# mLSTM log weights: rows spread over the partitions by DMA through device memory, in place of products on TensorE

## The chip, the cores and the metric

One NeuronCore of one Trainium2 chip runs the whole program. The metric is device time in microseconds (us): three runs of the kernel before took 2686.16, 2692.14 and 2697.73 us, median 2692.14. Engines are named as the profile names them: PE is TensorE, DVE is VectorE, ACT is ScalarE, POOL is GpSimd, SP is SyncE, which here only issues DMAs.

## The reference, cut to what matters

The program is two transformer-like blocks on 512 tokens of 1024 features. The first block has two layers; each begins with an input projection and feeds an mLSTM that runs over 128-token chunks, four heads, forward and backward. Layer 0 works on 768 tokens (512 and a context of 256), layer 1 needs outputs for 512 only. For one chunk and direction the reference computes:

```python
b = jnp.cumsum(fc, axis=-1)
a = b + m[..., None]
Dlog = b[..., :, None] - b[..., None, :] + ic[..., None, :]
Dlog = jnp.where(order, Dlog, -jnp.inf)
m_t = jnp.maximum(a, jnp.max(Dlog, axis=-1))
w_inter = jnp.exp(a - m_t)
s = jnp.einsum('bhtk,bhsk->bhts', qc, kc) * jnp.exp(Dlog - m_t[..., None])
num = w_inter[..., None] * jnp.einsum('bhtk,bhkv->bhtv', qc, C) + jnp.einsum('bhts,bhsv->bhtv', s, vc)
```

The factor `exp(Dlog - m_t)` is a 128 x 128 matrix per head, chunk and direction. Written with source token s on the partitions and target token t along the free dimension, its logarithm is a row in t, `b_t - m_t`, plus a column in s, `i_s - b_s`, plus a mask of 0 or -1e30. "Log weights" below are the row plus the mask; the column comes in as the bias of the exponential.

## The kernel before

**Tiles and stages.** A projection tile is 128 output features: `out = W^T x` over 8 feature tiles, each as three products of split operands (upper and lower halves, `w_hi`, `w_lo`, `XH`, `XL`). POOL splits each weight tile into `w_hi` and `w_lo` from a ring of four `raw` buffers that SP fills. Layer 0 does each tile in two parts, 512 tokens (24 products) and 256 tokens (24 products); layer 1 does tiles outside k and v for 512 tokens only, in two halves of 12 products. `in_projection` writes out by hand, tile by tile, what PE does: tiles 10 to 13 are v, 14 to 17 are q, tiles 18 and up are done in pieces inside the mLSTM. Between tile parts stand transposes, sums for the convolution branch (`conv_sum`: a sum of `AC`, later of its squares `YC`, over partitions) and the log weights. "Tile 15" below is position 15 of this order.

**Log weights.** `mlstm_steps(l)` lists 12 pairs of direction and chunk in each layer. All 12 give outputs in layer 0, 8 in layer 1: 20 in all. For each, `log_weights(l, i)` fills one PSUM bank, 3 or 4 in turn: one product with the identity writes the mask for four heads (line 1492), then four products (line 1495) with `selh`, a selector of 8 rows, copy row `4 d + h` of `ri` (8 rows x 768: 4 heads forward, 4 backward) to all 128 partitions and add it. ACT's `weights(i)` then writes `exp(PSUM + column)` to SBUF, four activations of 128x128 (line 1959), and sends back the bank.

**Order on ACT.** ACT's program is written by hand too: evacuate v and q tiles (`v_copy`, `q_tile`), `weights(0..3)`, `q_tile(1)`, `weights(4, 5)`, copy the convolution's mean to `MU`, `weights(6)`, `q_tile(2)`, `weights(7, 8)`, square `AC` into `YC`, the reciprocal root of the variance (`rstd`, two activations with a table load before each), `weights(9)`, `q_tile(3)`, `weights(10, 11)`, then the weighted keys `Ks` of the first step. PE's first `scores` wait for the last exponentials and for `q_tile(3)`.

**Order on DVE.** DVE ends the convolution's taps (`word` of line 2508 is its signal), waits for `MU`, subtracts it, waits for `rstd`, scales (line 2517), adds a bias (line 2521), and then begins the mLSTM with `weighted_scores(0)` (line 2554).

**DMA.** SP issues the weight loads in order, load n+4 when tile n is done, and among them in layer 0 batches of `modt` tiles that lie in `X` until PE has summed them (line 1382). The exponentials of layer 0 lie in `X` (`EP`), those of layer 1 in the unused context columns of `X` and `XF`.

## Time and profile before

| | |
|---|---|
| runs, device time | 2686.16, 2692.14, 2697.73 us, median 2692.14 |
| profiled execution, first to last instruction | 2693.6 us (its device time beyond the span is not listed) |
| mean granted TensorE clock | 0.984 of full |
| PE, POOL, DVE, ACT busy | 2576.0, 1583.7, 1391.5, 754.3 us |
| layer 0, tile 15 to first scores | 217.0 to 271.5 us |
| layer 1, tile 15 to first state update | 1174.5 to 1212.3 us |
| DMA | 255.57 MB, mean 95 GB/s |

A line of the page or of an answer names line, engine, operation and `out<-in`. Timeline lines begin with the start and the duration in us; brackets give the idle time of the engine before the instruction and what ended it. Matmuls are pipelined: each is listed with its whole latency, so the time that one takes from PE is the distance between starts. An fp32 product is listed as two passes, so `x8` on line 1495 is the four products of one `log_weights`.

### The profile page before, as it was taken

Reading aid. Unit: us, or ns where it says so; the run is one execution under the profiler, and the core shown is the slowest. Engines: PE = TensorE matmul, PEld = TensorE weight load, DVE = VectorE, ACT = ScalarE, POOL = GpSimd, SP = SyncE. Lnnn points to the kernel's source line nnn. Section 1 sums busy time; section 2 is a strip of 40 time slices with the busy share of each in tenths; the row PEclk is TensorE's granted clock in tenths of the full one; section 3 lists DMA queues with packets and bytes.
Section 4 is the critical chain, followed back from the end, with each engine's and each line's share of the span. In section 5 each row is a group of like instructions: output and inputs, shape, how many; then the busy total and the mean of one; then the engine's idle time right before and its main releaser. Section 6 shows DMA issues by size and latency. Waiting matters only on the chain.

```text
span 2693.6 us, 39857 instructions
## 1 busy us (share of the span) xinstructions
PE 2576.0 (96%) x14674; PEld 2116.4 (79%) x14674; DVE 1391.5 (52%) x2054; ACT 754.3 (28%) x1566; POOL 1583.7 (59%) x1668
## 2 busy tenths in 40 slices
PE   5999989999999999999899999999999999899998
PEld 4878978888888886878687877778878887677776
DVE  4862555662662858715533333354454445636744
ACT  3223353211111123234421212222222223324413
POOL 2532224675775665434587777776676765665464
PEclk9999999999999999999999999999999999999999
DMA  6341131332232322111133332433333332222221
GB/s 238 118 156 34 38 152 52 121 123 94 95 126 94 120 86 74 55 50 53 63 95 93 93 94 86 130 106 102 94 95 94 102 102 71 87 89 83 79 94 63
DMA packets 79263, 255.57 MB, mean 95 GB/s; under 512 B 9872, under 2 KB 13712, under 8 KB 78864
## 3 DMA queue, kind: packets, MB, share of 16 engines
q1 hardware_dynamic: 61280, 210.59, 24.3%
q10 hardware_dynamic: 17840, 43.03, 5.3%
q8 instruction: 95, 1.56, 0.2%
q14 instruction: 48, 0.39, 0.1%
HBM read 236.28 MB, written 2.10 MB: 88 GB/s over the span
## 4 chain that ended last, share of the span: by engine, by line
PE 42%; POOL 30%; issue 19%; DVE 5%; DMA 1%; ACT 1%; POOLq 1%; SPq 0%; DVEq 0%; ACTq 0%
POOL w_lo L427 17%; POOL w_hi L425 10%; PE PS L433 8%; PE PS L436 8%; PE PS L434 8%; PE PS L1508 4%; PE PS L1510 4%; PE PS L1509 4%; POOL word L420 2%; PE PS L1495 1%; DVE Z L2230 1%; PE PS L1382 1%; DMA modt<-in_wmod 1%; PE PS L1697 1%; DVE XL L2237 1%
## 5 line engine op out<-in xcount | busy, mean ns | idle before, releaser
L427 POOL TENSOR_TENSOR w_lo<-raw,w_hi 128x512 fp32r<-128x512 f32 (+1 forms) x662 | 957.3, 1446 | 55.2
L433 PE MATMUL PS<-XH,w_hi 128*128 128x512 f32 x2168 | 822.1, 379 | 32.6 <-DVE XL L2595 8.1
L434 PE MATMUL PS<-XL,w_hi 128*128 128x512 f32 x2168 | 794.0, 374 | 0.0
L436 PE MATMUL PS<-XH,w_lo 128*128 128x512 f32 x2168 | 745.0, 375 | 0.0
L420 POOL TENSOR_TENSOR word<-ones 128x1 f32<-128x1 f32 x331 | 103.2, 312 | 1040.4 <-PE PS L436 671.3
L425 POOL TENSOR_SCALAR w_hi<-raw 128x512 fp32r<-128x512 f32 (+1 forms) x662 | 533.4, 806 | 0.0
L433 PEld LDWEIGHTS PS<-XH,w_hi 128*128 128x128 f32 x2168 | 411.4, 190 | 140.9 <-issue 15.1
L434 PEld LDWEIGHTS PS<-XL,w_hi 128*128 128x128 f32 x2168 | 411.6, 190 | 74.1
L436 PEld LDWEIGHTS PS<-XH,w_lo 128*128 128x128 f32 x2168 | 381.4, 190 | 59.4
L1508 PE MATMUL PS<-XH,w_hi 128*128 128x512 f32 (+1 forms) x640 | 235.9, 369 | 10.6 <-DVE XL L2237 10.6
L1509 PE MATMUL PS<-XL,w_hi 128*128 128x512 f32 (+1 forms) x640 | 228.8, 357 | 0.0
L1510 PE MATMUL PS<-XH,w_lo 128*128 128x512 f32 (+1 forms) x640 | 228.7, 357 | 0.0
L2319 DVE TENSOR_TENSOR X<-X,Z 128x768 f32 (+3 forms) x60 | 87.8, 1464 | 226.3 <-ACT Z L1873 221.2
L433 PE MATMUL PS<-HH,w_hi 128*128 128x512 f32 (+1 forms) x528 | 188.4, 357 | 3.4 <-DVE HL L2662 3.4
L434 PE MATMUL PS<-HL,w_hi 128*128 128x512 f32 (+1 forms) x528 | 180.5, 357 | 0.0
L2283 DVE CUSTOM_DVE_ANT_0 cprod<-modv,cb 128x1024 f32<-128x1024 f32 x96 | 165.0, 1719 | 21.2 <-DMA modv<-in_wmod 18.1
L2657 DVE SCALAR_TENSOR_TENSOR Z<-TH,Z 128x768 f32<-128x768 f32 (+1 forms) x44 | 51.4, 1169 | 211.2 <-ACT Z L1854 209.2
L436 PE MATMUL PS<-HH,w_lo 128*128 128x512 f32 (+1 forms) x528 | 159.7, 356 | 0.0
L1508 PEld LDWEIGHTS PS<-XH,w_hi 128*128 128x128 f32 x640 | 125.1, 196 | 31.3 <-issue 11.1
L852 ACT ACTIVATE Z<-PS 128x512 f32<-128x512 f32 x99 | 58.9, 596 | 296.2 <-PE PS L436 292.5
L1510 PEld LDWEIGHTS PS<-XH,w_lo 128*128 128x128 f32 x640 | 124.5, 195 | 17.9
L1509 PEld LDWEIGHTS PS<-XL,w_hi 128*128 128x128 f32 x640 | 125.1, 195 | 15.9 <-issue 0.2
(329 smaller groups left out, 3230.6 us busy)
## 6 DMA issues: line engine op xcount, KB each, us to landing
raw<-in_wgu SPq DMA_DIRECT2D x88, 512.0 KB, 3.5
raw<-in_wa SPq DMA_DIRECT2D x80, 512.0 KB, 3.5
modt<-in_wmod SPq DMA_DIRECT2D x48, 512.0 KB, 9.8
raw<-in_win SPq DMA_DIRECT2D x48, 512.0 KB, 3.6
modv<-in_wmod ACTq DMA_DIRECT2D x48, 512.0 KB, 5.1
raw<-in_wdn SPq DMA_DIRECT2D x32, 512.0 KB, 3.5
QS<-Z ACTq DMA_DIRECT2D x100, 128.0 KB, 2.5
raw<-in_wout SPq DMA_DIRECT2D x16, 512.0 KB, 3.5
```

What stands on the lines that cost most here:

```text
L420: pool.tensor_tensor(word[:, 0:1], ones[:, 0:1], ones[:, 0:1], ALU.mult)
L425: pool.tensor_scalar(hi, src, 1.0, 0.0, ALU.mult, ALU.add).then_inc(s_hi, 1)
L427: pool.tensor_tensor(lo, src, hi.bitcast(FP32), ALU.subtract).then_inc(s_split, 1)
L433: pe.matmul(acc(s)[:, a:b], hi, rh[:, i, a:b], start=i == 0, stop=False)
L434: pe.matmul(acc(s)[:, a:b], hi, rl[:, i, a:b], start=False, stop=False)
L436: last = pe.matmul(acc(s)[:, a:b], lo, rh[:, i, a:b], start=False, stop=i == k - 1)
L852: return act.activation(Z[:, n % 4, 0:SEQ], acc(n)[:, 0:SEQ], ACT.Identity)
L1508: pe.matmul(out, hi, XH[:, i, a:b], start=first, stop=False)
L1509: pe.matmul(out, hi, XL[:, i, a:b], start=False, stop=False)
L1510: return pe.matmul(out, lo, XH[:, i, a:b], start=False, stop=i == KT - 1)
L2283: last = dve.tensor_tensor_reduce(out=cprod[:], in0=modv[slots + u][:], in1=cb[:, n, :], scale=0.5, scalar=0.0, op0=ALU.mult, op1=ALU.add, ...
L2319: dve.tensor_tensor(x, x, Z[:, s % 4, 0:w], ALU.add).then_inc(s_used, 1)
```

## The change

The rows no longer pass through PE. `ri` is stored once per layer to device memory (`rows_of_log_weights`) and read back by DMAs whose source repeats over 128 partitions; DVE adds the mask in SBUF; ACT takes the exponential in place. `identr`, `mskr`, `selh` and the instructions that made them go.

```diff
+            def spread_rows(l):
+                if l == 0:
+                    sp.wait_ge(s_mc, 10)
+                    for d in range(2):
+                        rows = rows_d[l, 4 * d:4 * d + 4].rearrange("(o h) t -> o (h t)", o=1)
+                        sp.dma_start(EP[:, d].rearrange("p h t -> p (h t)"), rows.to_broadcast([P, HEADS * T])).then_inc(s_rowb, 16)
+                    return
+                sp.wait_ge(s_tile, l * LAYER_TILES + Q_P)
+                for t, (d, j, first, gives) in enumerate(mlstm_steps(l)):
+                    if gives:
+                        rows = rows_d[l, 4 * d:4 * d + 4, j * P:(j + 1) * P].rearrange("(o h) t -> o h t", o=1)
+                        sp.dma_start(weights_of(l, t), rows.to_broadcast([P, HEADS, P])).then_inc(s_rowb, 16)
...
                     load(n0 + p, win_d[l, IN_ORDER[p]])
+                    if p == 13:
+                        sp.wait_ge(s_row, l + 1)
+                        sp.dma_start(rows_d[l], ri[:]).then_inc(s_rowd, 16)
+                    if p == 16 + l:
+                        sp.wait_ge(s_rowd, 16 * (l + 1))
+                        spread_rows(l)
...
-                pe.matmul(PS[:, bank, :].rearrange("p (h t) -> p h t", h=HEADS), identr[:], mskr[:, d:d + 1, :].to_broadcast([P, HEADS, P]),
-                          start=True, stop=False)
-                for h in range(HEADS):
-                    last = pe.matmul(PS[:, bank, h * P:(h + 1) * P], selh[:, 4 * d + h, :], ri[:, j * P:(j + 1) * P],
-                                     start=False, stop=h == HEADS - 1)
-                last.then_inc(s_w, 1)
...
                 if outputs_before(l, t) == outputs_before(l, 0):
-                    pe.wait_ge(s_e, outputs_before(l + 1, 0))
+                    pe.wait_ge(s_mod, 2)
+                    pe.wait_ge(s_cole, l + 1)
                     pe.wait_ge(s_evac, l * LAYER_TILES + U_P)
...
-                    act.wait_ge(s_w, o + 1)
+                    act.wait_ge(s_rowm, o + 1)
                     for h in range(HEADS):
-                        last = act.activation(out[:, h, :], PS[:, 3 + i % 2, h * P:(h + 1) * P], ACT.Exp, bias=gcol[:, j, 4 * d + h:4 * d + h + 1])
+                        last = act.activation(out[:, h, :], out[:, h, :], ACT.Exp, bias=gcol[:, j, 4 * d + h:4 * d + h + 1])
...
-                for i in range(4):
-                    weights(i)
                 q_tile(1)
-                weights(4)
-                weights(5)
+                for i in range(6):
+                    weights(i)
                 act.wait_ge(s_csum, l + 1)
                 act.activation(MU[:, 0:w], banks(6, 8)[:, 0:w], ACT.Copy, scale=1.0 / 256).then_inc(s_cmu, 1)
-                weights(6)
+                for i in range(6, 9):
+                    weights(i)
                 q_tile(2)
-                weights(7)
-                weights(8)
+                for i in range(9, 12):
+                    weights(i)
                 act.wait_ge(s_cd, l + 1)
...
-                weights(9)
                 q_tile(3)
-                weights(10)
-                weights(11)
...
+                for t, (d, j, first, gives) in enumerate(mlstm_steps(l)):
+                    if gives:
+                        o = outputs_before(l, t)
+                        dve.wait_ge(s_rowb, 32 + 16 * (outputs_before(l + 1, 0) - outputs_before(1, 0)))
+                        e = weights_of(l, t)
+                        dve.tensor_tensor(e, e, mskd[:, d:d + 1, :].to_broadcast([P, HEADS, P]), ALU.add).then_inc(s_rowm, 1)
```

`EP` becomes one tensor of 2 x 4 x 768 floats per partition over the same bytes of `X`. `scores` no longer wait for the exponentials, since `weighted_scores` on DVE waits for each (`s_e`) itself.

On ACT, in layer 0, this stood from the copy of the mean (`MU<-PS`) to the squares (`YC<-AC`); `EP` are the weights, `qfm` a q tile:

```order
L2018 ACTIVATE MU<-PS 128x768 [waits conv_sum_done]
L1959 ACTIVATE EP_194<-PS,gcol 128x128 [waits log_weights_done]
L1959 ACTIVATE EP_194<-PS,gcol 128x128 x3
L1908 ACTIVATE qfm<-PS,bcol 128x512 [waits gemm_tile_done,gelu_made,sgu_mixed]
L1910 ACTIVATE qfm<-PS,bcol 128x256
L1959 ACTIVATE EP_195<-PS,gcol 128x128 [waits log_weights_done]
L1959 ACTIVATE EP_195<-PS,gcol 128x128 x3
...
L2024 ACTIVATE YC<-AC 128x1536 [waits conv_centred]
L1808 ACT_TABLE_LOAD
```

and this stands there now, with three sets of weights where one stood ahead of the q tile, and three where two stood behind it:

```order
L1997 ACTIVATE MU<-PS 128x768 [waits conv_sum_done]
L1940 ACTIVATE EP<-EP,gcol 128x128 [waits spread_rows_masked]
L1940 ACTIVATE EP<-EP,gcol 128x128 x3
...
L1891 ACTIVATE qfm<-PS,bcol 128x512 [waits gemm_tile_done,gelu_made,sgu_mixed]
L1893 ACTIVATE qfm<-PS,bcol 128x256
L1940 ACTIVATE EP<-EP,gcol 128x128 [waits spread_rows_masked]
L1940 ACTIVATE EP<-EP,gcol 128x128 x3
...
L2004 ACTIVATE YC<-AC 128x1536 [waits conv_centred]
L1791 ACT_TABLE_LOAD
```

The last three sets, which stood behind `rstd`, are ahead of the squares now; nothing but the q tile is left between `rstd` and the weighted keys.

On DVE, in layer 0, between the end of the convolution's taps (`word`) and the subtraction of the mean there was nothing:

```order
L2311 SCALAR_TENSOR_TENSOR AC<-YC,pc,AC 128x241 [waits dve_chain]
L2508 TENSOR_TENSOR word<-ones 128x1 [waits dve_chain]
L2512 TENSOR_TENSOR AC<-AC,MU 128x768 [waits conv_mean_made]
L2512 TENSOR_TENSOR AC<-AC,MU 128x768
L2517 SCALAR_TENSOR_TENSOR AC<-AC,pc,MU 128x768 [waits conv_rstd_made,conv_centred]
L2517 SCALAR_TENSOR_TENSOR AC<-AC,pc,MU 128x768
```

and there are the twelve mask additions now, each of which waits until all rows are spread:

```order
L2288 SCALAR_TENSOR_TENSOR AC<-YC,pc,AC 128x241 [waits dve_chain]
L2484 TENSOR_TENSOR word<-ones 128x1 [waits dve_chain]
L2491 TENSOR_TENSOR EP<-EP,mskd 128x4x128 [waits rows_spread_over_partitions] x12
L2495 TENSOR_TENSOR AC<-AC,MU 128x768 [waits conv_mean_made]
L2495 TENSOR_TENSOR AC<-AC,MU 128x768
L2500 SCALAR_TENSOR_TENSOR AC<-AC,pc,MU 128x768 [waits conv_rstd_made,conv_centred]
L2500 SCALAR_TENSOR_TENSOR AC<-AC,pc,MU 128x768
```

On SP, in layer 1, the eight spreading DMAs stand between the loads of tiles 17 and 18 (`raw`); before, those two loads followed one another:

```order
L1269 DMA raw_49<-in_win 128x1024 [waits gemm_tile_done]
L1269 DMA raw_50<-in_win 128x1024 [waits gemm_tile_done]
L1286 DMA X<-rows_of_log_weights 128x4x128 [waits gemm_tile_done,rows_stored]
L1286 DMA X<-rows_of_log_weights 128x4x128 x3
L1286 DMA XF<-rows_of_log_weights 128x4x128 x4
L1269 DMA raw_51<-in_win 128x1024 [waits gemm_tile_done]
L1269 DMA raw_52<-in_win 128x1024 [waits gemm_tile_done]
```

In layer 0 two DMAs of 128x3072 floats stand in the same way between the loads of tiles 16 and 17.

## Rows read from the trace of the kernel before

**Rows 1.** Section 1 of the page, the engine that bounds.

```profile
PE 2576.0 (96%) x14674; PEld 2116.4 (79%) x14674; DVE 1391.5 (52%) x2054; ACT 754.3 (28%) x1566; POOL 1583.7 (59%) x1668
```

**Rows 2.** Timeline of TensorE: start us, duration us, engine, line, operation, count, [idle before it].

```profile
216.45 0.81 PE L1398 MATMUL PS<-ident,Z 128*128 128x128 f32 x6
217.02 0.47 PE L1492 MATMUL PS<-mskr,identr 128*128 128x512 f32 x1
...
220.02 0.50 PE L1508 MATMUL PS<-XH,w_hi 128*128 128x512 f32 x1
...
225.71 0.40 PE L1492 MATMUL PS<-mskr,identr 128*128 128x512 f32 x1
...
243.23 2.74 PE L1503 MATMUL PS<-AC,ones 128*128 128x512 f32 x8
...
271.54 0.79 PE L1665 MATMUL PS<-qfm,kfm 128*128 128x128 f32 x2 [1.23 <-ACT EP L1959]
```

**Rows 3.** All instructions of line 1495: ns min/median/max.

```profile
L1495 PE MATMUL PS<-row,selh x160: 270/270/372, 217.4 to 1202.3; 8*128 8x128 f32 x160
```

**Rows 4.** Three stretches: start:end, length, busy us by engine, granted clock, DMA share.

```profile
229.00:232.30 3.30, 3.30 (x19) 3.30 (x18) 0.00 (x0) 0.89 (x4) 0.00 (x0) 0.51 0.00 0
217.00:271.54 54.54, 53.31 (x272) 42.40 (x270) 8.23 (x8) 24.82 (x64) 15.34 (x19) 0.89 0.13 39
1174.45:1212.30 37.85, 35.61 (x155) 26.16 (x154) 3.50 (x6) 18.91 (x47) 13.53 (x17) 0.91 0.17 49
```

**Rows 5.** Timeline of ScalarE in layer 0.

```profile
233.39 0.69 ACT L1908 ACTIVATE qfm<-PS,bcol 128x512 f32<-128x512 f32 x1 [3.50 <-PE PS L1510]
...
234.61 1.15 ACT L1959 ACTIVATE EP<-PS,gcol 128x128 f32<-128x128 f32 x4 [0.17 <-PE PS L1495]
...
246.00 0.81 ACT L2018 ACTIVATE MU<-PS 128x768 f32<-128x768 f32 x1 [8.67 <-PE PS L1503]
...
254.28 1.50 ACT L2024 ACTIVATE YC<-AC 128x1536 f32<-128x1536 f32 x1
...
263.08 0.90 ACT L1808 ACTIVATE MU<-PS,eps_c 128x768 f32<-128x768 f32 x1 [6.00 <-PE PS L1503]
...
271.36 1.28 ACT L2044 ACTIVATE Ks<-ktm,KD 128x128 f32<-128x128 f32 x4
```

**Rows 6.** Timeline of ScalarE: the same shape read from SBUF.

```profile
368.43 4.80 ACT L2082 ACTIVATE EP<-EP,hq 128x128 f32<-128x128 f32 x16
```

**Rows 7.** Timeline of VectorE in layer 0.

```profile
217.84 1.11 DVE L2508 TENSOR_TENSOR word<-ones 128x1 f32<-128x1 f32 x1
...
266.24 1.95 DVE L2517 SCALAR_TENSOR_TENSOR AC<-AC,pc,MU 128x768 f32<-128x768 f32 x2 [17.57 <-ACT MU L1809]
268.22 2.54 DVE L2521 TENSOR_SCALAR AC<-AC,pc 128x768 f32<-128x768 f32 x2
273.70 0.69 DVE L2554 TENSOR_TENSOR EP<-PS,EP 128x512 f32<-128x512 f32 x1 [2.94 <-issue]
```

**Rows 8.** DMA issues of the page: KB each, us to landing.

```profile
X<-in_xT SPq DMA_DIRECT2D x1, 3072.0 KB, 11.9
```

**Rows 9.** The DMA view of 2294 to 2302 us: 40 slices, packets by size.

```profile
GB/s 0 0 0 0 0 0 102 0 225 184 246 287 369 389 476 318 323 358 374 384 369 353 364 328 374 389 384 379 399 405 389 394 451 451 348 389 451 451 348 389
DMA packets 1394, 2.37 MB, mean 296 GB/s; under 512 B 48, under 2 KB 1072, under 8 KB 1394
...
PWR<-in_plep SPq DMA_DIRECT2D x1, 1024.0 KB, 6.3
```

**Rows 10.** Timelines of SyncE (layer 1) and TensorE (layer 0): where the transfers may start.

```profile
1167.82 0.33 SPq L1268 DMA_DIRECT2D raw<-in_win  x1
...
182.34 3.70 PE L1382 MATMUL PS<-modt,cz 128*32 128x128 f32 x128
```

**Rows 11.** Timelines of ScalarE and TensorE in layer 1.

```profile
1209.32 0.63 ACT L1809 ACTIVATE MU<-MU 128x512 f32<-128x512 f32 x1
...
1212.32 0.98 PE L1697 MATMUL PS<-vtm,Ks 128*128 128x129 f32 x3 [2.27 <-issue]
```

More of the change, by code:

```diff
@@ L227, in build_program @@
         mskd = place("mskd", [P, 2, P])
-        mskr = place("mskr", [P, 2, P], FP32R, addr=addr_of["mskd"])
-        identr = place("identr", [P, P], FP32R)
         ST = [place(f"ST{d}", [P, HEADS, P + 1]) for d in range(2)]
@@ L291, in build_program @@
         r2 = place("row4", [8, T], addr=addr_of["vtm"])
-        selh = place("selh", [8, 8, P], addr=addr_of["tho"] + 2 * T * 4)
         NUM = [place(f"NUM{e}", [P, HEADS, P + 1], addr=addr_of["YC"] + e * 4 * (HEADS * (P + 1) + 4)) for e in range(2)]
         XF = place("XF", [P, KT, T], addr=addr_of["XH"])
-        EP = [place(f"EP{i}", [P, HEADS, P], addr=addr_of["X"] + i * 4 * HEADS * P) for i in range(2 * NJ)]
+        EP = place("EP", [P, 2, HEADS, T], addr=addr_of["X"])
+        rows_d = nc.dram_tensor("rows_of_log_weights", (DEPTH, 8, T), FP32).ap()
         grow = place("grow", [16, T], addr=addr_of["Z"] + 3 * T * 4)
@@ L303, in weights_of @@
             if l == 0:
-                return EP[t][:]
+                d, j = mlstm_steps(l)[t][0:2]
+                return EP[:, d, :, j * P:(j + 1) * P]
             i = outputs_before(l, t) - outputs_before(l, 0)
@@ L381, in build_program @@
         s_cole = sem("columns_made")
-        s_w = sem("log_weights_done")
+        s_rowd = sem("rows_stored")
+        s_rowb = sem("rows_spread_over_partitions")
+        s_rowm = sem("spread_rows_masked")
         s_e = sem("weights_made")
@@ L1327, in _ @@
             pool.wait_ge(s_one, 3)
-            pool.wait_ge(s_id, 16)
-            pool.tensor_scalar(identr[:], ident[:], 1.0, 0.0, ALU.mult, ALU.add).then_inc(s_one, 1)
             for l in range(DEPTH):
@@ L1334, in _ @@
                     split_weights(pool, n0 + n)
-                    if l == 0 and n == 3:
-                        pool.wait_ge(s_const, 16 * 4)
-                        pool.tensor_scalar(mskr[:], mskd[:], 1.0, 0.0, ALU.mult, ALU.add).then_inc(s_one, 1)
                 with pool.Fori(0, 2) as i:
@@ L1473, in columns @@
                 last.then_inc(s_cols, 1)
-            def log_weights(l, i):
-                steps = [s for s in mlstm_steps(l) if s[3]]
-                if i >= len(steps):
-                    return
-                d, j = steps[i][0:2]
-                o = outputs_before(l, 0) + i
-                bank = 3 + i % 2
-                if i < 2:
-                    pe.wait_ge(s_one, 5)
-                    pe.wait_ge(s_mod, 2)
-                    pe.wait_ge(s_cole, l + 1)
-                    pe.wait_ge(s_mixu, 2 * (l + 1))
-                else:
-                    pe.wait_ge(s_e, o - 1)
-                if i == 0 and l:
-                    pe.wait_ge(s_tile, l * LAYER_TILES + Q_P)
-                pe.matmul(PS[:, bank, :].rearrange("p (h t) -> p h t", h=HEADS), identr[:], mskr[:, d:d + 1, :].to_broadcast([P, HEADS, P]),
-                          start=True, stop=False)
-                for h in range(HEADS):
-                    last = pe.matmul(PS[:, bank, h * P:(h + 1) * P], selh[:, 4 * d + h, :], ri[:, j * P:(j + 1) * P],
-                                     start=False, stop=h == HEADS - 1)
-                last.then_inc(s_w, 1)
             def conv_sum(l, src, signal):
@@ L1641, in in_projection @@
                 conv_sum(l, YC, s_cvar)
-                log_weights(l, 9)
                 second_half(l, 17)
-                log_weights(l, 10)
-                log_weights(l, 11)
             def piece(l, i):
@@ L1703, in inside @@
                 o = outputs_before(l, t)
+                if o == outputs_before(l, 0):
+                    pe.wait_ge(s_mixu, 2 * (l + 1))
                 pe.wait_ge(s_p, o + 1)
@@ L1953, in weights @@
                     o = outputs_before(l, 0) + i
-                    act.wait_ge(s_w, o + 1)
-                    if i == 4 and l:
-                        act.wait_ge(s_tile, n0 + Q_P)
+                    act.wait_ge(s_rowm, o + 1)
                     out = weights_of(l, mlstm_steps(l).index(steps[i]))
                     for h in range(HEADS):
-                        last = act.activation(out[:, h, :], PS[:, 3 + i % 2, h * P:(h + 1) * P], ACT.Exp, bias=gcol[:, j, 4 * d + h:4 * d + h + 1])
+                        last = act.activation(out[:, h, :], out[:, h, :], ACT.Exp, bias=gcol[:, j, 4 * d + h:4 * d + h + 1])
                     last.then_inc(s_e, 1)
@@ L2106, in _ @@
                             if p == O_P:
-                                act.wait_ge(s_w, outputs_before(l + 1, 0))
+                                act.wait_ge(s_rowd, 16 * (l + 1))
                             in_tile(p, tho[:, p - O_P], ACT.Tanh, 0.5)
@@ L2475, in _ @@
                 dve.wait_ge(s_cols, l + 1)
-                dve.tensor_copy(selh[:], ident[0:8, 0:8].rearrange("p (r c) -> p r c", c=1).to_broadcast([8, 8, P]))
                 dve.tensor_tensor(KD[:, 0].rearrange("p j e -> p (j e)"), PS[:, 3, 0:8 * NJ], gcol[:].rearrange("p j e -> p (j e)"), ALU.add)
```

11 lines of the change are left out of this document (1 added, 10 removed).

## Prediction

> **What bounds the kernel now.** I read section 1 of the page first: PE is busy for 96% of the span [rows 1], so a microsecond taken from PE is worth one unless something else is late there. Then the timeline of PE where the log weights stand: they interrupt q tiles 15 to 17, two sets at a time. In layer 0 a pair runs from 217.02 to 220.02, and the following half tile to 225.71; the stretch ends at 271.54 with the first scores, after an idle time of 1.23 us for which ACT's last exponentials are named [rows 2]. Line 1495 has 160 passes, which are 20 sets of 8 [rows 3]. [...] The timelines of ACT and DVE then show who will be late once PE is faster [rows 5, 7].
>
> **What goes from PE.** A pair costs 3.00 us, a set 1.50, so 12 sets in layer 0 take 18.0 us and 8 in layer 1 take 12.0 [rows 2]. The low clock comes on top. The first such stretch, 229.0 to 232.3, comes right after four sets whose products load only 8 rows; there are three such stretches in layer 0's 54.54 us and two in layer 1's 37.85 [rows 4]. Each is about 3.2 us long; at full clock it would be half that, so five of them cost about 1.6 us each, 8 us. With the idle 1.2 us in front of the scores PE could give back 18.0 + 12.0 + 8.0 + 1.2 = 39 us. It will not get all of it, because ACT's list is long.
>
> **What ACT's list allows, layer 0.** The new order puts all 12 sets of exponentials ahead of the squares. Prices: a q tile 233.39 to 234.61 less the wait of 0.17 shown there, 1.05 us; the mean 0.8; the squares 1.5; `rstd` from 263.08 to the 266.24 at which DVE uses it, 3.1 [rows 5, 7]. Four exponentials from PSUM start 0.26 us apart (four in 1.15 with a last one of 0.37), four activations of this shape from SBUF 0.30 apart (16 in 4.80) [rows 5, 6]. The new ones read SBUF, so a set is taken at 1.2 us, with 1.04 as the other end. [...]
>
> The walk. Tile 15 starts at 217.02 instead of 220.02; its first part takes 5.69 (220.02 to 225.71), the second, with half the columns, 2.85, so it ends at 225.6 [rows 2]. Adding 0.3 for the hand-over and 1.05 for the q tile, exponentials start at 226.9; six sets end at 234.1. PE meanwhile does the first part of tile 16 (231.3) and the convolution's sum, 2.77 from its start at 243.23 to the read at 246.00 [rows 2, 5]: 234.0, so the mean does not wait. Mean 234.9, three sets 238.5, q tile 239.55, three sets 243.15, squares 244.65. PE has finished the first part of tile 17 at about 242.2 and idles 2.6 us; this is the new wait. The sum of squares then needs 2.77 at full clock. Behind idle times of 1.23 and 2.27 us the trace has the lower clock [rows 2, 4, 11], so I add 1.2, half of what the sum could lose: 248.8. `rstd` ends at 251.9. DVE scales and adds its bias in 4.5 (266.24 to 268.22 + 2.54) [rows 7] and reaches `weighted_scores(0)` at 256.5, while PE's scores, which now need only the q tile, start at 253.2 and are not late. Before, that instruction started at 273.70 [rows 7]. Layer 0 gains 17.2 us; with 1.04 us per set and full clock 19.6, with the whole loss of clock 16.0.
>
> **DVE's twelve additions.** One writes 128x512 like the product at 273.70, 0.69 us [rows 7], so 12 take about 8 us. They start behind `word`, at 218.95, and end at 227; DVE has nothing else until the mean at 234.9. The first must precede 226.9, which it does by 7 us if the rows are there. They cost nothing. Without that cover each would add its 0.69.
>
> **The rows' arrival, layer 0.** SP may issue when PE has summed the last `modt` tiles, 182.34 + 3.70 = 186.0 [rows 10]. The nearest row is the load of the same 24 KB per partition of `X`, 3072 KB in 11.9 us [rows 8]: landing at 198. All must be there 0.9 us ahead of 226.9; 40 us are there for 12, and the load queued behind them is used a tile and a half later. Cost zero, down to some 86 GB/s. The store of the row is issued three tiles earlier and hides too.
>
> **Layer 1.** The same walk for 512 tokens, parts that scale by tokens at two thirds. Tile 15 starts at 1174.45 [rows 4], ends at 1180.15; q tile to 1181.1; six sets 1188.3; mean 1188.9; two sets 1191.3; q tile 1192.0; squares 1193.0; PE, free since about 1190, sums to 1195.6 (1.85 plus hand-over and 0.6 of low clock); `rstd`, whose table loads do not scale, 2.7: 1198.3. Before it ended at 1209.32 + 0.63 = 1209.95, and the first update followed 2.4 later at 1212.32 [rows 11]; that tail stays. Gain 11.6; at 1.04 per set and full clock 13.6.
>
> Here the rows may be late. They cannot be issued before 1167.82 + 0.33 = 1168.15, behind a weight load [rows 10], and are eight DMAs with 4096 pieces of 512 bytes, 2.10 MB. The nearest row has 1 KB pieces: 1024 KB, queued behind 512 KB, landed in 6.3 us; at 374 GB/s, the middle of the busy slices, its own bytes take 2.8, so 3.5 us are start, completion and the load ahead, and a piece costs 16 x 1024 / 374 = 44 ns of one engine [rows 9]. If a 512-byte piece costs the same, 256 of them per engine take 11.3 us; if bytes count, 5.6. Landing is 1177.3 to 1183.0. One addition and a hand-over (0.9) later the exponentials may start: 1178.2 to 1183.9 against the 1181.1 at which ACT is free. That is 0 to 2.8 us; I take 1.2, toward the packet price, since the row shows packets at close to full rate only down to 1 KB. [...] Layer 1 gains 10.4.
>
> **Sum.** 17.2 + 10.4 = 27.6 us. The profiled execution's span is 2693.6 us; its time outside the span is not listed, and none of it changes. The span is 1.5 above the median of the runs, 2692.1, from which I subtract: 2664.5, rounded 2665. `selh`, `identr` and `mskr` go from DVE and POOL where neither is waited for. Everything later runs as before, shifted.
>
> **Rivals.**
> - *All of PE's time comes back.* For it: 96% busy. Against it: the walk, in which ACT holds back the squares for 2.6 to 3 us of PE in each layer. It needs cheaper exponentials and no low clock at all. 2692 - 39 = 2653. Chance 0.10.
> - *The spread of layer 1 is slow.* 128 partitions read the same few rows of device memory, which nothing in the trace does. At 100 GB/s the 2.10 MB take 21 us, landing is 1192.7, ACT waits 12.5 us instead of 1.2, and the time is 2676. Chance 0.15.
> - *The spread is slow in both layers, and the kernel slower.* Layer 0 waits 3.15 MB / rate - 36.5, layer 1 2.10 MB / rate - 8.5, which together eat 28.8 us at 71 GB/s. At 55 GB/s they are 20.7 and 29.7, and the time is 2692 + 50 - 29 = 2713. Decisive is whether the repeated source is served at a sixth of the rate of ordinary loads (about 374 GB/s); against it, 12 KB pieces in layer 0. Chance 0.06.
> - *Nothing moves*, because what PE gives up turns into a wait I have not seen (the weight split on POOL, a buffer): 2692. POOL is busy for 59% of the span [rows 1], and in the two stretches for 15.34 of 54.54 and 13.53 of 37.85 us [rows 4], so it has room for shorter ones. Chance 0.04.
>
> **How the numbers follow.** The forecast has 0.65; its own range is 2659 to 2672, from the ends of the walks and 3 us of scatter of a median of runs that differ by 11.5. Reaching to the first two rivals for eight chances in ten gives 2654 to 2679. A change under 0.5%, 13.5 us, can't be told from none. Faster by more than that are the forecast, the first rival and two thirds of the second: 0.85. Within it are the rest of the second and the fourth: 0.09. Slower: 0.06.
>
> **What would show it.** No line with `selh`, and PE from tile 15 to the first scores in about 36 us instead of 54.5. A PE idle time of 2 to 3 us ahead of the sum of `YC`, ended by ACT's squares. Exponentials 0.30 us apart. DVE's additions in layer 0 ahead of any use, `EP` landing about 12 us after issue. In layer 1 the wait of DVE's first `X` addition, ended by the DMA, between 1177 and 1183. Granted clock in tiles 16 and 17 at full level. Wrong it would be if the exponentials wait for DVE for long, or if the low-clock pieces stay where only dense products are left.

## The result, and the profile after

The changed kernel takes 2660.23 us in the median of 4 runs (2658.91 to 2662.45), the kernel before beside it 2693.72 (4 runs, 2686.16 to 2697.73). The ratio is 0.988, with a 95% interval of 0.986 to 0.990: faster by 33.5 us, or 1.2%, and by 27 us at the least. The profiled execution took 2662.45 us with a span of 2660.6, 33.0 less than that of before. Section 1 of the page:

```profile
PE 2539.9 (95%) x14494; PEld 2087.6 (78%) x14494; DVE 1407.3 (53%) x2072; ACT 754.9 (28%) x1566; POOL 1590.8 (60%) x1666
```

180 instructions and 36 us of busy time are gone from TensorE (PE) against [rows 1]; the additions and the transfers stand on VectorE (DVE) and in the queues instead. TensorE's timeline in layer 0, from the transposes ahead of tile 15 to the first weighted scores (columns as in [rows 2]):

```profile
218.05 0.82 PE L1414 MATMUL PS<-ident,Z 128*128 128x128 f32 x6
...
232.70 2.74 PE L1495 MATMUL PS<-AC,ones 128*128 128x512 f32 x8
...
245.68 2.85 PE L1495 MATMUL PS<-YC,ones 128*128 128x512 f32 x8 [1.78 <-ACT YC L2004]
...
252.72 0.46 PE L1646 MATMUL PS<-qfm,kfm 128*128 128x128 f32 x2 [1.32 <-ACT qfm L1893]
253.88 1.13 PE L1678 MATMUL PS<-vtm,Ks 128*128 128x129 f32 x8
...
258.15 1.77 PE L1646 MATMUL PS<-qfm,kfm 128*128 128x128 f32 x8 [3.14 <-DVE EP L2537]
259.71 1.93 PE L1693 MATMUL PS<-vtm,EP 128*128 128x129 f32 x8
```

No `selh` is left. From tile 15's start to the first scores it is 34.1 us, where [rows 2] had 54.5. Three idle times are new: 1.78 us ahead of the sum of `YC`, ended by the squares on ScalarE (ACT); 1.32 ahead of the scores, ended by the q tile; and 3.14 ahead of the second scores, ended by DVE. The timeline of ACT, which answers to [rows 5]:

```profile
228.35 7.13 ACT L1940 ACTIVATE EP<-EP,gcol 128x128 f32<-128x128 f32 x24
235.48 0.81 ACT L1997 ACTIVATE MU<-PS 128x768 f32<-128x768 f32 x1
236.19 3.61 ACT L1940 ACTIVATE EP<-EP,gcol 128x128 f32<-128x128 f32 x12
...
240.64 3.62 ACT L1940 ACTIVATE EP<-EP,gcol 128x128 f32<-128x128 f32 x12
244.15 1.48 ACT L2004 ACTIVATE YC<-AC 128x1536 f32<-128x1536 f32 x1
...
250.78 0.84 ACT L1792 ACTIVATE MU<-MU 128x768 f32<-128x768 f32 x1
```

24 exponentials in 7.13 us and 12 in 3.62 are 0.297 and 0.302 us each, the pitch of [rows 6]; they start 9.7 us behind tile 15's start and never wait for DVE. The squares end at 245.63, and PE starts 0.05 later. The timeline of DVE, against [rows 7]:

```profile
218.71 0.60 DVE L2484 TENSOR_TENSOR word<-ones 128x1 f32<-128x1 f32 x1
219.23 9.92 DVE L2491 TENSOR_TENSOR EP<-EP,mskd 128x512 f32<-128x512 f32 x12
...
251.72 3.35 DVE L2500 SCALAR_TENSOR_TENSOR AC<-AC,pc,MU 128x768 f32<-128x768 f32 x2 [13.57 <-ACT MU L1792]
255.11 2.38 DVE L2504 TENSOR_SCALAR AC<-AC,pc 128x768 f32<-128x768 f32 x2
257.41 0.68 DVE L2537 TENSOR_TENSOR EP<-PS,EP 128x512 f32<-128x512 f32 x1
```

The twelve additions are over at 229.15. The scaling and the bias ahead of the weighted scores at 257.41 took 3.35 + 2.38 = 5.7 us, where [rows 7] had 4.5. The windows, against [rows 4]:

```profile
218.62:252.72 34.10, 31.01 (x164) 25.20 (x162) 13.32 (x17) 25.09 (x64) 15.59 (x18) 1.00 0.16 49
258.10:261.40 3.30, 3.25 (x17) 3.25 (x17) 2.42 (x3) 2.08 (x5) 0.00 (x0) 0.56 0.00 0
1155.97:1181.04 25.07, 20.68 (x83) 14.91 (x82) 12.89 (x14) 18.98 (x47) 16.16 (x17) 1.00 0.39 118
```

Granted clock 1.00 in both stretches, where it was 0.89 and 0.91. The one piece with a lower clock is the 3.3 us behind the idle time of 3.14: 0.56, and 0.50 from 259.0 to 261.4. The transfers as SyncE issues them, in layer 0 (one row) and layer 1:

```profile
187.43 0.80 SPq L1280 DMA_DIRECT2D EP<-rows_of_log_weights  x2
...
1149.77 2.03 SPq L1286 DMA_DIRECT2D X<-rows_of_log_weights  x4
1151.84 5.01 SPq L1286 DMA_DIRECT2D XF<-rows_of_log_weights  x4
```

In layer 0 the issue is at 187.43. The two transfers landed 6.8 and 10.1 us after their issues (8.5 is the median that the DMA view gives), so the rows lie ready some 21 us ahead of their first use at 219.23. In layer 1 the first DVE addition shows the landing:

```profile
1161.17 2.92 DVE L2491 TENSOR_TENSOR X<-X,mskd 128x512 f32<-128x512 f32 x4 [14.10 <-DMA XF<-rows_of_log_weights]
1164.01 5.09 DVE L2491 TENSOR_TENSOR XF<-XF,mskd 128x512 f32<-128x512 f32 x4
```

DVE stood 14.10 us and was let go by the last transfer at 1161.17, 5.2 us behind tile 15's start at 1155.97. ACT started its exponentials 1.3 us later, and waited neither for the transfer nor for DVE:

```profile
1162.50 4.78 ACT L1940 ACTIVATE X<-X,gcol 128x128 f32<-128x128 f32 x16
1167.19 2.45 ACT L1940 ACTIVATE XF<-XF,gcol 128x128 f32<-128x128 f32 x8
...
1173.00 1.06 ACT L2004 ACTIVATE YC<-AC 128x1024 f32<-128x1024 f32 x1
```

And PE in layer 1, where the squares hold it back; the idle 2.18 us ahead of the first update stood there before too, as 2.27 [rows 11]:

```profile
1155.40 0.82 PE L1414 MATMUL PS<-ident,Z 128*128 128x128 f32 x6
...
1174.11 1.98 PE L1495 MATMUL PS<-YC,ones 128*128 128x512 f32 x4 [2.21 <-ACT YC L2004]
...
1181.04 1.13 PE L1678 MATMUL PS<-vtm,Ks 128*128 128x129 f32 x8 [2.18 <-issue]
```

### The profile page after: what moved, and what is told of

It is laid out like the page before. It is cut to its first block, busy times and chain, and to the rows that moved or that the text cites. A ratio compares the mean times of both kernels' runs of the same rounds, so it can differ in the third digit from the quotient of the medians.

```text
span 2660.6 us, 39519 instructions
## 1 busy us (share of the span) xinstructions
PE 2539.9 (95%) x14494; PEld 2087.6 (78%) x14494; DVE 1407.3 (53%) x2072; ACT 754.9 (28%) x1566; POOL 1590.8 (60%) x1666
## 4 chain that ended last, share of the span: by engine, by line
PE 41%; POOL 30%; issue 19%; DVE 5%; ACT 2%; DMA 1%; POOLq 1%; SPq 0%; ACTq 0%; DVEq 0%
POOL w_lo L428 17%; POOL w_hi L426 10%; PE PS L434 8%; PE PS L437 8%; PE PS L435 8%; PE PS L1500 4%; PE PS L1502 4%; PE PS L1501 4%; POOL word L421 2%; DVE Z L2207 1%; PE PS L1398 1%; DMA modt<-in_wmod 1%; DVE XL L2214 1%; DVE X L1166 1%; ACT EP L1940 1%
## 5 line engine op out<-in xcount | busy, mean ns | idle before, releaser
L2260 DVE CUSTOM_DVE_ANT_0 cprod<-modv,cb 128x1024 f32<-128x1024 f32 x96 | 165.6, 1725 | 20.8 <-DMA modv<-in_wmod 17.6
## 6 DMA issues: line engine op xcount, KB each, us to landing
modt<-in_wmod SPq DMA_DIRECT2D x48, 512.0 KB, 10.1
```

Of the source, the lines that this page charges most:

```text
L2260: last = dve.tensor_tensor_reduce(out=cprod[:], in0=modv[slots + u][:], in1=cb[:, n, :], scale=0.5, scalar=0.0, op0=ALU.mult, op1=ALU.add, ...
```

## The experiments

One measure serves for all of them, since it is free of what happens elsewhere in the span: from the start of the six transposes ahead of tile 15 to the start of the first key update (`vtm,Ks`), by the timelines of PE. The mean clock is of that stretch. The stretches come from one traced execution of each kernel, the median from all its executions. The measure leaves out what follows the update in layer 0: from there to the first product with `EP` it is 3.4 us before, 5.8 in the changed kernel, 1.9 with full rows and 3.1 with the products kept.

The kernels ran on several chips, and the kernel before is not equally fast on them: beside the changed kernel it had a median of 2693.7 us, beside full rows, products kept, ACT's order and the later spread 2693.3, beside mask on one column, early squares and weighted first 2689.3, and beside the three marked "again" 2689.1. So medians are compared within one of these groups, and across them the ratios are.

| kernel | layer 0, us | clock | layer 1, us | clock | median us | ratio to before, 95% |
|---|---|---|---|---|---|---|
| before | 56.95 | 0.89 | 38.44 | 0.91 | 2693.3 | |
| changed | 35.83 | 1.00 | 25.64 | 1.00 | 2660.2 | 0.986 to 0.990 |
| full rows (from before) | 47.21 | 1.00 | 32.14 | 1.00 | 2672.4 | 0.992 to 0.995 |
| products kept | 55.09 | 0.90 | 38.35 | 0.91 | 2690.2 | 0.998 to 1.000 |
| ACT's order of before | 37.27 | 0.96 | 27.60 | 0.94 | 2660.0 | 0.987 to 0.990 |
| spread a tile later | 35.84 | 1.00 | 32.98 | 0.90 | 2666.5 | 0.989 to 0.993 |
| mask on one column | 35.82 | 1.00 | 25.65 | 1.00 | 2661.1 | 0.988 to 0.991 |
| early squares | 33.78 | 1.00 | 24.24 | 1.00 | 2663.3 | 0.988 to 0.991 |
| weighted first | 33.77 | 1.00 | 23.16 | 1.00 | 2656.9 | 0.986 to 0.989 |
| changed, again | 35.83 | 1.00 | 28.90 | 0.94 | 2664.0 | 0.989 to 0.992 |
| early squares, again | 33.79 | 1.00 | 23.15 | 1.00 | 2659.6 | 0.987 to 0.990 |
| weighted first, again | 33.78 | 1.00 | 25.41 | 1.00 | 2658.4 | 0.987 to 0.990 |

**Does the low clock come from the 8-row products?** From the kernel before:

```diff
-    last = pe.matmul(PS[:, bank, h * P:(h + 1) * P], selh[:, 4 * d + h, :], ri[:, j * P:(j + 1) * P],
+    last = pe.matmul(PS[:, bank, h * P:(h + 1) * P], ident[:], tri[:, d, :],
...
-    ... ACT.Exp, bias=gcol[:, j, 4 * d + h:4 * d + h + 1])
+    ... ACT.Exp, bias=ident[:, j:j + 1])
```

> The kernel before, with one edit: the 8-row selector products (weights `selh`, 8 rows, on 8 rows of `ri`) become products of the same number and output shape over all 128 rows (`ident` on `tri`), and the exponentials take a fixed column as bias; so the log weights, and with them the output, are other numbers, while every instruction, wait and transfer stays. Theory A (the low clock in tiles 15 to 17 comes from products that use 8 of 128 rows): the granted clock stays near 1.00 from tile 15's start to the first weighted scores, the stretch from tile 15 to the first piece of L0 shrinks from 60.7 us to about 53, and the time falls by about 8 us to some 2685. Theory B (the low clock comes from the idle times of TensorE around the products or from something else in these tiles): granted clock 0.89 and 60.7 us as before, time 2692 +- 3. If B holds, only the absence of the work in these tiles, not the shape of the products, gave the clock back.

Measured: 2672.39 us, 21 less than before by the medians and 17 by the ratio (13 to 22 by its interval), with TensorE still doing 20 sets of as many products. The clock is at 1.00 in both layers, so theory A holds and B falls. The first scores still stand behind 1.23 us of idle time here, as in [rows 2], and the clock behind it is 1.00 (259.9 to 263.0), where it was 0.50 before (271.5 to 274.9). Windows of the stretches, columns as in [rows 4]:

```profile
213.90:235.30 21.40, 21.40 (x135) 19.04 (x133) 2.50 (x4) 9.56 (x29) 8.01 (x10) 1.00 0.16 50
235.30:249.67 14.37, 14.37 (x84) 12.13 (x83) 1.83 (x2) 7.94 (x17) 3.94 (x5) 1.00 0.12 38
1158.33:1190.47 32.14, 29.97 (x159) 24.22 (x158) 3.46 (x6) 19.17 (x47) 13.75 (x18) 1.00 0.18 58
```

The gain is larger than the 8 us expected, because a set has become cheaper too. Its rows in this kernel, from PE's timeline:

```profile
215.59 0.47 PE L1492 MATMUL PS<-mskr,identr 128*128 128x512 f32 x1
215.91 1.05 PE L1495 MATMUL PS<-tri,ident 128*128 128x128 f32 x8
216.72 0.47 PE L1508 MATMUL PS<-XH,w_hi 128*128 128x512 f32 x1
```

The second set runs from 215.59 to 216.72: 1.13 us, not the 1.50 of [rows 2]. Of the 0.37 us, 0.28 lie in the eight passes and 0.09 in the mask product ahead of them. Over 20 sets that is 7.4 us at full clock. The two stretches shrank by 9.7 + 6.3 = 16.0 us, and the 3.4 us between the first update and the first product with `EP` in layer 0 by another 1.6, half of a low-clock piece. 17.6 less 7.4 leaves 10.2 for the clock. I had put the clock at 8 us; and of the 30 us for the products some 7 were the price of their having 8 rows.

**Are TensorE's products the whole gain?** Into the changed kernel, at the places of before, with nobody reading them:

```diff
+    pe.matmul(PS[:, bank, :]..., identr[:], identr[:]....to_broadcast([P, HEADS, P]), start=True, stop=False)
+    for h in range(HEADS):
+        pe.matmul(PS[:, bank, h * P:(h + 1) * P], tri[0:8, 0, :], ri[:, j * P:(j + 1) * P], start=False, stop=h == HEADS - 1)
```

> The changed kernel with TensorE's 20 sets of products kept at their old places in its program (mask product and four 8-row products, into PS banks 3 and 4), which nobody reads; transfers, mask additions and exponentials stay as changed. Theory A (the gain is TensorE's products and the low clock they bring): the stretch from tile 15 to L0's first piece goes from 42.7 back to 58-61 us, L1's from 25.1 to 35-38 us, the clock of tile 15's stretch from 1.00 to about 0.9, time 2690 (2685 to 2697). Rival R (the gain comes from ACT, which reads SBUF instead of PSUM and has a new order, or from TensorE's waits on it): products beside the new order cost their bare 30 us at most partly, time 2670 to 2680, clock near 1.00.

Measured: 2690.15 us, within 0.2% of before. The stretches are back to 55.1 and 38.4 us, against 57.0 and 38.4 before, and so is the low clock, in the windows of both:

```profile
216.91:272.00 55.09, 55.09 (x285) 44.24 (x283) 17.21 (x20) 27.29 (x68) 16.74 (x20) 0.90 0.12 39
1171.93:1210.28 38.35, 36.18 (x159) 26.68 (x158) 8.34 (x14) 19.29 (x47) 13.71 (x18) 0.91 0.26 80
```

The rival falls: as long as the products stay, reading SBUF, the new order of ACT and the transfers together are worth the 1.9 us by which layer 0 is shorter than before. Nor does the low clock need idle time of PE here: it is 0.83 from 225.0 to 245.0, and PE is busy for all of layer 0's 55.09 us. This kernel also settles what makes a set dear. It loads the same weights for all four products of a set, as the kernel with full rows does, but 8 rows of them. PE's timeline:

```profile
217.48 0.48 PE L1506 MATMUL PS<-identr 128*128 128x512 f32 x1
217.88 1.15 PE L1509 MATMUL PS<-row,tri 8*128 8x128 f32 x8
218.97 0.50 PE L1506 MATMUL PS<-identr 128*128 128x512 f32 x1
```

The eight passes take 1.09 us (217.88 to 218.97), 0.136 each, where the passes over 128 rows take 0.81 (215.91 to 216.72, above), 0.101 each. In the kernel before, where the weights change from product to product, the eight passes took 1.08 (217.43 to 218.51 on its timeline). The clock was 1.00 in all three places. So the number of rows makes the difference here, not the changing of weights.

**Is the new order of ACT needed?**

```diff
+                for i in range(4):
+                    weights(i)
                 q_tile(1)
-                for i in range(6):
-                    weights(i)
+                weights(4)
+                weights(5)
...
-                for i in range(6, 9):
-                    weights(i)
+                weights(6)
                 q_tile(2)
-                for i in range(9, 12):
-                    weights(i)
+                weights(7)
+                weights(8)
...
+                weights(9)
                 q_tile(3)
+                weights(10)
+                weights(11)
```

> The changed kernel with ACT's order of before in tiles 15 to 17 (sets 0 to 3, q tile 1, sets 4 and 5, centering, set 6, q tile 2, sets 7 and 8, squares, set 9, and so on) in place of the new one. Theory A (the new order is not where the gain comes from; the squares stand behind nine exponential sets instead of twelve here): TensorE's wait ahead of the second convolution sum shrinks from 1.8 us to 0-0.5 in L0, first piece of L0 0.5 to 2 us earlier, L1 between 1 us earlier and 1 us later, time 2658 to 2661. Rival R (the order is needed, since without it the q tiles or key scaling come late and TensorE stands): a wait of 3 us or more appears on the qfm tile at the first scores of a layer, time 2664 to 2668.

Measured: 2660.01 us, as the changed kernel. Of its five executions the traced one took 8493.13 us, three times the others, and the record does not show why; the other four took 2659.43 to 2662.71 us. That trace says nothing of the stretches, so the kernel ran once more.

> The changed kernel with ACT's order of before, once more for its trace. Its time stands already: 2660.01 us, as the changed kernel's. Theory A: TensorE's wait for the squares in L0 falls from 1.8 us to under 0.5, and what is gained there is lost at another place of tiles 16 or 17 or in the scatter; Rival R: a wait of 1 us or more on the qfm tile at the first scores, which takes the place of the one for the squares.

Measured: 2659.8 us in two executions, and for layer 0 the rival's picture. PE's waits there (engine, tile and line, what it waited for, us, times, longest):

```profile
PE PS L1646 <- ACT qfm L1893: 2.5, 1, 2.5
PE PS L1678 <- ACT Ks L2025: 1.6, 1, 1.6
```

The wait for the squares is gone and 2.5 + 1.65 us for the q tile and the key scaling stand in its place; layer 0's stretch is 1.4 us longer, not shorter. But the first product with `EP` comes 40.8 us behind the transposes, 41.7 in the changed kernel, since nothing waits 3.1 us behind the update. Layer 1 loses 2.0 us, and among its waits of PE is the one for the squares:

```profile
PE PS L1495 <- ACT YC L2005: 2.5, 1, 2.5
```

The lower clock follows these waits of 2.5 us in both layers: 0.50 from 250.0 to 256.0 and 0.70 from 1166.6 to 1169.3, 0.96 and 0.94 over the stretches. So the order matters for 1 or 2 us in either direction, and the whole time can't tell. Of theory A the time came and the gain in layer 0, but only behind the update and in spite of the rival's waits; in layer 1 it had allowed for 1 us of loss, not 2. Of the rival the waits came, the 2664 us or more did not.

**Are the transfers hidden?**

```diff
-    if p == 16 + l:
+    if p == (17, 18)[l]:
```

> The changed kernel with the spread of the rows issued later: L0 at step 17 instead of 16, L1 at step 19's predecessor (18) instead of 17, that is one tile later in both layers (about 23 us in L0, about 12 us in L1). Theory A (L0's landing has 22 us in hand, L1's only about 1): L0's rows land about when the additions start, the stretch from tile 15 to L0's first piece stays within 1 us of 42.7; in L1 the exponentials start later by the part of the shift that the 1 us does not cover, 5 to 11 us, and the first update comes as much later: time 2666 to 2671. Rival R (transfers are hidden in both layers, TensorE's chain decides): within 1 us of the changed kernel, 2659 to 2661. Rival S (the transfers compete with the weights' and state's loads, so later is better): below 2658.

Measured: 2666.47 us, 6.2 more than the changed kernel and within theory A's range. Layer 0 stays to 0.01 us. In layer 1 the transfer decides the addition; of the waits of DVE in that stretch the longest is

```profile
DVE X L2491 <- DMA XF<-rows_of_log_weights: 20.5, 1, 20.5
```

and of those of PE, through ACT's list, the one for the squares:

```profile
PE PS L1495 <- ACT YC L2004: 7.9, 1, 7.9
```

The stretch is 7.3 us longer than the 25.6 of the changed kernel. In layer 0 DVE's first addition did wait 1.9 us for the rows, but ACT begins its exponentials 7 us later, so nothing came of it. Layer 0's transfer has a tile in hand, and layer 1's has nothing like it: in the changed kernel it lands 1.3 us before ACT comes free.

**Are the additions hidden?**

```diff
-    dve.tensor_tensor(e, e, mskd[:, d:d + 1, :].to_broadcast([P, HEADS, P]), ALU.add)
+    dve.tensor_tensor(e[:, :, 0:1], e[:, :, 0:1], mskd[:, d:d + 1, 0:1].to_broadcast([P, HEADS, 1]), ALU.add)
```

> The changed kernel with the mask added to one column of 128 of each block instead of all of them (mask left out), and exponentials with scale 0 and a fixed bias so that no number grows; so the weights, and the output, are other numbers, while the count of instructions, the waits and the transfers stay. It takes away VectorE's time for the twelve and eight additions (9.9 us in L0, 8.0 us in L1). Theory A (VectorE's additions are hidden): from the transposes of tile 15 to the first key update 35.8 us in L0 as now (+-0.3) and 25.6 in L1 (+-0.6), time 2659 to 2661. Rival D (they are on the path, or slow GpSimd's splitting of the weights and so TensorE): several us less, time below 2656.

The exponentials have scale 0 and a fixed bias here, and the mask is left out of the result. Measured: 35.82 and 25.65 us, and 2661.10 us, a time that can't be told from the changed kernel's, as the intervals of the ratios overlap. In the traced execution VectorE's additions cost nothing. The changed kernel once more, below, shows a case in layer 1 where they did.

**Can the new waits be had back?** Squares ahead of part of the exponentials: in layer 0 behind seven sets instead of twelve, in layer 1 behind five instead of eight, with the last two and three sets behind the first key scaling. The cut shows layer 0:

```diff
-    for i in range(6, 9): weights(i)
+    for i in range(6, 7): weights(i)
     q_tile(2)
-    for i in range(9, 12): weights(i)
     (squares)
+    for i in range(7, 10): weights(i)
...
     weighted_keys(0)
+    for i in range(10, 12): weights(i)
```

> The changed kernel with ACT's squares for the second convolution sum drawn ahead of part of the exponentials (L0: sets 0 to 5, centering, set 6, q tile 2, squares, sets 7 to 9, rstd, q tile 3, key scaling, sets 10, 11; L1: sets 0 to 2, centering, 3, 4, q tile 2, squares, rstd, q tile 3, key scaling, 5 to 7). Theory A (what keeps the gain below TensorE's 39 us are the 1.8 and 2.2 us that TensorE waits for the squares): both waits go, L0's stretch from tile 15's transposes to the first update shrinks from 35.8 to about 34 us and L1's from 25.6 to about 23.4; nothing else comes late; time about 2656. Rival R (the wait moves: the q tile or the key scaling comes late at the first scores, or the weights' last sets come late at the first pieces): the stretch stays within 0.5 us, and a wait of about 2 us shows on another line; time 2659 to 2661.

> The kernel with the early squares, once more. Its first trace gave 33.8 and 24.2 us for the two stretches (1.8 and 1.4 less than the changed kernel), but a half clock right behind the first update of L1, which cost 1.9 us. Theory A (the clock falls behind an idle of TensorE when no other idle came shortly before, so the wait that was removed had covered for it): the low piece behind L1's first update is there again, and the time is the changed kernel's within 1.5 us. Rival R (the low piece was scatter): no low piece, time about 3 us below the changed kernel.

Measured: layer 0 shorter by 2.0 us both times, the squares' wait gone. Layer 1 by 1.4 and 2.5, with 0.8 us of that wait left the first time and none the second. But behind the first update of layer 1 the first run had the lower clock, and the second, with the same 2.2 us of idle ahead of the update, not. The window behind that update in the first (the last three numbers are granted clock, DMA share and GB/s):

```profile
1176.81:1181.20 4.39, 4.39 (x16) 3.69 (x17) 2.23 (x4) 4.39 (x14) 3.14 (x3) 0.61 0.20 80
```

and in the second:

```profile
1176.91:1181.20 4.29, 3.91 (x20) 3.05 (x20) 2.07 (x3) 4.29 (x14) 3.17 (x3) 1.00 0.16 65
```

So that piece is scatter and my cause for it (that the removed wait had covered for it) fell. Mask on one column has it too, with a clock of 0.68 behind the update, though its squares' wait stands as in the changed kernel. The two medians of 2663.3 and 2659.6 decide nothing: the first was 7 us above what I expected, the second 4.4 below the changed kernel on the same chip, and the intervals of the ratios overlap both times. Then, on VectorE in layer 0, the first weighted scores between the two scalings of `AC`:

```diff
+    if l == 0 and f == 0:
+        (waits for the scores and the exponentials)
+        dve.tensor_tensor(weights_of(0, 0), PS[:, 3, :]..., weights_of(0, 0), ALU.mult).then_inc(s_p, 1)
```

> As the kernel with the early squares, and on VectorE in L0 the first weighted scores between the two scalings of the convolution instead of behind both. Theory A (TensorE's 3.1 us of idle ahead of the second scores wait for VectorE, which does the convolution's scaling first, and the half clock of the next 3 us follows from that idle): the wait falls to 1 us or less, the clock of the following stretch is 1.00, L0's way from first update to first weighted piece shrinks from 5.8 us to about 2 to 3.5, time 2 to 3 us below the kernel with the early squares, about 2653. Rival R (the scaling is then late at the convolution's transposes): within 1 us of the kernel with the early squares.

> The kernel with early squares and the first weighted scores ahead of the second scaling, once more. If its 2656.9 us was more than the chip's scatter, it is again 2 to 4 us below the changed kernel; if not, within 1.5 us of it.

DVE's timeline in layer 0, in the second of these runs:

```profile
248.06 1.36 DVE L2502 SCALAR_TENSOR_TENSOR AC<-AC,pc,MU 128x768 f32<-128x768 f32 x1 [11.52 <-ACT MU L1792]
250.27 0.69 DVE L2508 TENSOR_TENSOR EP<-PS,EP 128x512 f32<-128x512 f32 x1 [0.84 <-PE PS L1646]
250.88 1.07 DVE L2502 SCALAR_TENSOR_TENSOR AC<-AC,pc,MU 128x768 f32<-128x768 f32 x1
```

The weighted scores now stand at 250.27, between the two scalings. PE's wait ahead of the second scores is gone; 2.27 us stand instead ahead of the product with `EP`, for which DVE must first copy `ST`, and from update to that product it is 4.3 us, not 5.5 to 6.1, though more than the 2 to 3.5 expected. The clock behind it is 1.00 (254.0 to 260.0), as expected. With the early squares the way from the transposes to that product is 38.1 us, in both runs, against 41.7 and 41.4 in the changed kernel: 3.3 to 3.6 us. In layer 1 the squares' wait was 2.0 us again in the second run. As to the whole times, 2658.4 is 5.6 below the changed kernel's 2664.0 on the same chip. The 2656.9 of the first run came on a chip where the kernel before was itself 4.4 us faster, and by the ratio it is 1 us better than the changed kernel. The intervals overlap both times, so a faster kernel is likely but not shown by the whole times.

**The changed kernel once more.**

> The changed kernel as it is, once more beside the two below on one chip, since their times came from another chip than its own and differ by less than that allows. Expected 2660 us (2658 to 2663), and in the trace the same stretches: 35.8 us from tile 15's transposes to the first update in L0, 25.6 in L1, full clock in both.

Measured: 2664.01 us against 2689.13, a gain of 25 us (22 to 31), and 1 us above the range expected. The traced execution is the slowest of the four, 2671.21 us against 2662.53 to 2664.40. Its layer 0 is the same to the hundredth. Its layer 1 is 3.3 us longer, where I had expected the same 25.6: PE waited 3.8 us for the squares, and the lower clock followed. Its timeline there, and the window behind:

```profile
1174.27 2.79 PE L1495 MATMUL PS<-YC,ones 128*128 128x512 f32 x4 [3.83 <-ACT YC L2004]
...
1174.00:1182.85 8.85, 6.40 (x17) 3.84 (x17) 2.98 (x4) 5.96 (x10) 1.95 (x3) 0.81 0.10 23
```

The additions on the four `X` sets had 5.49 us this time instead of 2.92 and began 6.8 us behind the transposes instead of 5.8, so ACT waited for DVE three times, 1.4 us in all. Here the additions were not hidden. DVE's timeline in layer 1:

```profile
1160.73 5.49 DVE L2491 TENSOR_TENSOR X<-X,mskd 128x512 f32<-128x512 f32 x4 [15.11 <-DMA XF<-rows_of_log_weights]
1166.14 2.48 DVE L2491 TENSOR_TENSOR XF<-XF,mskd 128x512 f32<-128x512 f32 x4
```

The rest of this execution's length, 6.8 us behind the first update of layer 1, is in code that the change doesn't touch. In the last attention PE waited five times for `QB`, by the waits of 2430 to 2530 us:

```profile
PE PS L704 <- DVE QB L1075: 4.0, 5, 0.8
```

The same view of the changed kernel's first trace has one such wait, of 0.2 us; the first trace of weighted first has 4.0 us again. What sets these waits was not tried.

## Why the prediction was right, step by step

The forecast was 2665 us, 27.6 us of gain, in a range of 2659 to 2672. Measured were 2660.2 and, once more, 2664.0 us, gains of 33.5 and 25.1. Of the 8.4 us between the two gains 4.6 are the kernel before, which differs by that much between the two chips. The mechanism was as forecast, and some terms were mis-sized in both directions.

- *What goes from PE, 39 us.* Shown by the products kept: with them the kernel is back at 2690. The five low-clock pieces at 1.6 us, half of 3.2 by the 0.51 of [rows 4], are 8; full rows gave about 10. That they come from the 8-row products I had only concluded from where they stood; full rows (clock 1.00 in layer 0) and products kept (0.90) show it. What I had missed is that the low row count also makes the products themselves dear, 0.37 us a set. It did not touch the sum, as I took the price of a set from the row.
- *ACT's list, layer 0.* Exponentials at +9.7 us behind tile 15's start (walk: +9.9), 0.30 each as chosen, mean at +16.9 (+17.1), squares at +25.5 (+26.1), PE idle 1.8 (2.6). The walk charged the PSUM-to-SBUF difference rightly: 0.26 us apart from PSUM before, 0.297 from SBUF now.
- *The term for the low clock behind PE's new idle, 1.2 us in layer 0 and 0.6 in layer 1.* Wrong: the clock stayed at 1.00 behind 1.78 and 2.21 us. I had taken the lower clock (0.50) behind the 1.23 us in [rows 2] as the price of that idle time; with full rows it was 1.00 behind the same 1.23 us. DVE's scaling and bias took 1.2 us longer than in [rows 7], which I had not foreseen. The two errors cancel, by luck; with the squares 0.6 us ahead of the walk the weighted scores came at +38.8 instead of +39.5, and layer 0 gained 17.9 us, not 17.2.
- *DVE's twelve additions, layer 0's landing.* Both cost nothing, as shown by one column and by the later spread. The additions took 0.83 us each, not 0.69. The later of the two transfers landed 10.1 us after its issue, not 12.
- *PE's wait for DVE behind the first update in layer 0.* The walk has DVE ready 3.3 us after PE's scores begin and puts no price on what follows. PE stood for 3.14 us, and the clock behind it was 0.56 for 3.3 us.
- *The landing in layer 1, 1.2 us.* Mis-sized for the first execution: landing 5.2 us behind tile 15's start, in the middle of the 2.9 to 8.6 that the two prices gave, but the exponentials could start 6.5 behind it, when ACT was free (walk: 6.7). The wait was 0. In the second traced execution ACT had three waits for DVE, 0.69 + 0.42 + 0.27 = 1.4 us, at a time when the rows landed 1.0 us later and the additions were slow; how much is due to which was not tried. With the lower clock behind it (0.81) that was 3.3. Whether bytes or pieces set the price is not settled, since the landing lies between the two. Layer 1 gained 12.8 us (25.64 against 38.44) instead of 10.4: 1.2 for the wait, 0.6 for the clock and the rest from a walk that was some tenths too slow.
- *The sum.* 17.9 + 12.8 = 30.7 of the 33.0 between the two spans. Another 1.5 lie right behind layer 1's first update: to the next update it was 5.27 us at a clock of 0.70 before and 3.78 at 1.00 after. That may be chance, as the products kept had full clock there too. What is left is less than the 6.8 us that two executions of the changed kernel differ by behind layer 1's first update.
- *The rivals.* All of PE's 39 us: no, the gain stayed 5.5 below it, and the new idle times for the squares, the q tile and DVE add up to 8.5 us. A slow spread: no, 3.15 MB had landed about 10.5 us after the first issue. Nothing moves: no.

## What to carry to other kernels

Look for products that load few rows in a kernel that TensorE bounds. Here those over 8 rows cost more per pass (0.136 us against 0.101) and brought the clock down for the dense products around them (0.89 over layer 0's stretch, 1.00 without them); as many products over all rows in their place (with other numbers as their result) took 17 to 21 us less. Moving them off TensorE gave some 12 more by the medians, and it was nearly free because the transfer (in layer 0 with 21 us in hand) and the additions fell into the idle time of their engines. When a walk along the engines' lists gives the new waits, read the transfer with the least in hand first: here a tile later cost 6 us in layer 1 and nothing in layer 0.

## What was not expected of the hardware

- Passes of a 128x128 product over 8 rows started 0.136 us apart (products kept), over 128 rows 0.101 (full rows), with nearly the same duration in the records (medians 0.270 and 0.275 us); only the distance to the next start shows it.
- The low clock did not go with idle time alone in these stretches. It fell without any idle time among the 8-row products (products kept, layer 0, 0.90). It stayed at 1.00 behind idle times of 1.8 and 2.2 us, and behind 2.3 in weighted first, and fell behind 2.5 (ACT's order of before, 0.50 in layer 0 and 0.70 in layer 1), 3.1 (layer 0, 0.56) and 3.8 us (layer 1, second execution, 0.69 from 1174.3 to 1177.0). Behind the 2.2 to 2.3 us ahead of layer 1's first update it fell in 3 of 12 traces: before 0.70, early squares 0.61, mask on one column 0.68.
- Of the twelve additions of 128x512 on VectorE in layer 0 one took 0.68 us in the median and 0.83 in the mean, and in layer 1 the four on `X` took 0.73 each in one execution and 1.37 in another. Within them single ones went to 1.78 us while GpSimd split weights: the long ones of layer 0 lie between 219.8 and 224.3, and GpSimd's splitting lasts from 218.69 to 223.79. That GpSimd is the cause is read from the records' overlap, not tried.
- Issues of transfers with 512-byte pieces held SyncE's queue: eight of them 7.1 us (1149.77 to 1156.85), and the last one landed 4.3 us after that. So most of the way from first issue to last landing is the time of the issues; a change of either alone was not tried.
